# First mixer: q and k rotated through one gathered tile each, and scaled by 1/rms on eviction

## The chip, the cores and the metric

The kernel runs on one core of a Trainium2 chip. The metric is the time of one execution on the device in microseconds (us). Engines: TensorE (PE, matmuls; PEld its weight loads), VectorE (DVE), ScalarE (ACT), GpSimd (POOL), and SyncE (SP), which only issues transfers. ACTq is ScalarE's instruction queue. L1188 is line 1188 of the kernel before.

## What is computed

Two decoder layers over 512 tokens of width 1024, in float32. Each layer: token mixer, cross-attention into 256 memory tokens, SwiGLU feed-forward, each behind an RMS norm and with a residual. The first layer's mixer, cut to what matters:

```python
proj = h @ w_in                       # h: rms-normed input
x_br, y_br, q, k, v = jnp.split(proj, list(AB_SPLITS), axis=-1)
rec = rg_lru(causal_depthwise_conv(x_br, ...), ...) * jax.nn.gelu(y_br)
q = partial_rope(heads(q), cos, sin)  # 8 heads of 64; only the first 16 of a head's 64 rows turn
k = partial_rope(heads(k), cos, sin)
att = dilated_attention(q, k, heads(v))
return jnp.concatenate([rec, att], axis=-1) @ w_out

def partial_rope(x, cos, sin):        # ROT_DIM = 16, half = 8
    x1, x2 = x[..., :half], x[..., half:ROT_DIM]
    return concatenate([x1 * cos - x2 * sin, x2 * cos + x1 * sin, x[..., ROT_DIM:]])
```

## The kernel before

Activations lie transposed: 128 partitions of features, 512 columns of tokens. Every large product is done in three matmuls of 128x512 (`product`, L606, L609, L610): a float32 operand is split into a high and a low part, and high x high, high x low and low x high are summed. A weight unit (256 rows of 512 columns) is loaded by SyncE into one of four slots (L404), GpSimd writes its high part (L537), VectorE its low part (`low_part`, L1188). A unit's load waits until TensorE has begun the unit three before it. `low_to(u)` in VectorE's stream writes low parts up to unit u; where these calls stand is an order written out by hand. The engines run their streams in order and meet at semaphores only.

The norm's 1/rms is not applied to the input but behind the product, since it is one factor a token: `rstd` holds it for all 128 partitions.

Order of TensorE in the first mixer: in_x (two groups of four output tiles, 4 weight units each), in_q (one group: four tiles of q), four gate groups (one unit each; they need the convolved x in high and low parts, `conv` and `conv_low` on VectorE), the turning of the normed memory (L764), in_k, in_v (by token), then the mixer: 12 score steps, three for each of four pairs of heads, with halves of the y projection (`half_columns`) between them. PSUM has 8 banks: even-numbered groups use banks 0 to 3, odd ones 4 to 7, so a group waits until the one two before it has been read (`s_free`). in_q's banks are wanted by the second gate group, in_k's by the mixer.

q and k before: ScalarE copies each tile from PSUM unscaled (`raw_tiles`, L1892). VectorE turns each of the eight tiles by itself (`qk_tile`, `rotate`, L1255 to L1258: shuffle, times cosines, times sines, sum, each over 128 partitions, of which 32 change) with tables `cos_r` and `sin_r`, which are the cosines and sines times 1/rms (L1383, L1384) and hold 1 and 0 in the rows that don't turn, so that this also scales the tile. q's four tiles are turned between the gated products of the gates (`gated`, L1424); k's first two in the middle of the recurrence (`recur`, L1446 and L1447), the other two in mixer steps 1 and 4 (the score step of pair p waits only for tile p of k).

ScalarE's stream: the raw copies of q; per gate group two sigmoids for r (L1904) and two for i (L1907), the latter into two buffers that `gated` must have read; the memory's high parts; exponentials, tanh and roots of the decay; the raw copies of k; v's evictions (L1927); then the mixer's exponentials (L1946), copies and GeLUs.

The second layer rotates q and k in another way: ScalarE issues transfers that gather the 16 turning rows of each head into a packed tile, 32 rows a tile of q or k (L1995), VectorE turns the packed tile once (`rotate_pack`, L1560 to L1563) with tables in packed form that SyncE loads ahead of that layer, and ScalarE issues the transfers back (`spread`, L2006).

## Time and profile before

| | |
|---|---|
| time, median of 3 runs | 1348.42 us (1346.99 to 1348.92) |
| the profiled execution | 1347.47 us, span 1345.6 us |
| busy share of the span | PE 99%, PEld 81%, DVE 56%, ACT 26%, POOL 24% |
| granted TensorE clock | 1.0 over the run |
| moved by DMA | 129.85 MB, mean 96 GB/s |

The profile is of one execution. The page has the busy shares and the costliest groups of instructions; the trace behind it is asked for the timeline of one engine, its waits (who released it), the instructions of one line, and busy time by stretches. Spans are from the first instruction; about 1.9 us of the execution's time lie outside. A share of 99% on TensorE says that it is the engine to watch, and the few microseconds in which it waits say where.

### The profile page before, as it was taken

The page shows a single profiled execution, that of the slowest core. Times are in us where ns is not written, and L with a number is a line of the kernel's source. Part 1 is how long each engine was busy: PE and PEld are TensorE (multiplying, and loading weights), DVE is VectorE, ACT ScalarE, POOL GpSimd, SP SyncE. Part 2 cuts the span into 40 slices and gives each one's busy share as a digit, 9 for nine tenths or more (in the row PEclk, how much of TensorE's full clock was granted, in tenths as well). Part 3 has the DMA queues.
Part 4 walks back from the last instruction along what each step waited for, and adds up shares of the span by engine and source line. Part 5 has one row for each costly group of instructions (what it writes and reads, how often), then busy time and mean ns, then how long its engine had stood idle before and what let it go on. Part 6 is the DMA issues. An engine that isn't in the chain of part 4 may idle for free.

```text
span 1345.6 us, 17355 instructions
## 1 busy us (share of the span) xinstructions
PE 1329.2 (99%) x6432; PEld 1089.1 (81%) x6432; DVE 750.6 (56%) x1089; ACT 351.8 (26%) x733; POOL 321.8 (24%) x358
## 2 busy tenths in 40 slices
PE   8999999999999999999999999999999999999998
PEld 7877778888788888888888878888788888888886
DVE  6997975446685443234444668557674443334432
ACT  5338355312441110001111246523321110001112
POOL 2122125311421121111211126424222111122110
PEclk9999999999999999999999999999999999999999
DMA  6332222233333232233323341122323333333222
GB/s 208 102 95 79 94 70 76 78 104 93 108 95 101 94 94 94 98 104 95 94 94 112 99 128 57 64 95 82 106 94 94 94 96 104 99 94 94 94 94 94
DMA packets 95985, 129.85 MB, mean 96 GB/s; under 512 B 6416, under 2 KB 60944, under 8 KB 95920
## 3 DMA queue, kind: packets, MB, share of 16 engines
q1 hardware_dynamic: 94448, 127.31, 29.6%
q10 hardware_dynamic: 1472, 1.64, 0.5%
q8 instruction: 45, 0.74, 0.2%
q14 instruction: 20, 0.16, 0.0%
HBM read 125.19 MB, written 2.10 MB: 95 GB/s over the span
## 4 chain that ended last, share of the span: by engine, by line
PE 86%; DVE 8%; issue 2%; DMA 1%; POOL 1%; ACT 0%; SPq 0%; ACTq 0%; DVEq 0%; POOLq 0%
PE ps L606 24%; PE ps L609 24%; PE ps L610 24%; DVE xc L1389 1%; PE ps L1160 1%; PE ps L1156 1%; PE ps L1159 1%; DVE w_lo L1188 1%; DMA raw<-in_w_in 1%; PE ps L732 1%; PE ps L707 1%; PE ps L984 1%; PE ps L1002 1%; PE ps L1017 1%; DVE xc L1447 1%
## 5 line engine op out<-in xcount | busy, mean ns | idle before, releaser
L1188 DVE TENSOR_TENSOR w_lo<-raw,w_hi 128x1024 fp32r<-128x1024 f32 x226 | 281.6, 1246 | 425.5 <-POOL w_hi L537 423.9
L537 POOL TENSOR_SCALAR w_hi<-raw 128x1024 fp32r<-128x1024 f32 x226 | 249.9, 1106 | 922.5 <-DMA raw<-in_w_gate_up 403.3
L606 PE MATMUL ps<-z_hi,w_hi 128*128 128x512 f32 x1040 | 408.8, 393 | 3.3 <-ACTq L1910 1.8
L610 PE MATMUL ps<-z_hi,w_lo 128*128 128x512 f32 x1040 | 404.8, 389 | 0.0
L609 PE MATMUL ps<-z_lo,w_hi 128*128 128x512 f32 x1040 | 404.8, 389 | 0.0
L606 PEld LDWEIGHTS ps<-z_hi,w_hi 128*128 128x128 f32 x1040 | 195.2, 188 | 50.8 <-issue 8.3
L609 PEld LDWEIGHTS ps<-z_lo,w_hi 128*128 128x128 f32 x1040 | 195.3, 188 | 41.2 <-issue 1.4
L610 PEld LDWEIGHTS ps<-z_hi,w_lo 128*128 128x128 f32 x1040 | 195.2, 188 | 40.6
L606 PE MATMUL ps<-f_hi,w_hi 128*128 128x512 f32 x528 | 208.0, 394 | 1.8 <-issue 1.1
L610 PE MATMUL ps<-f_hi,w_lo 128*128 128x512 f32 x528 | 205.6, 389 | 0.0
L609 PE MATMUL ps<-f_lo,w_hi 128*128 128x512 f32 x528 | 205.5, 389 | 0.0
L2117 ACT ACTIVATE ff_g<-ff_g 128x512 f32<-128x512 f32 x44 | 27.7, 632 | 349.0 <-DVE ff_g L1710 349.0
L606 PEld LDWEIGHTS ps<-f_hi,w_hi 128*128 128x128 f32 x528 | 99.1, 188 | 24.0 <-issue 2.8
L609 PEld LDWEIGHTS ps<-f_lo,w_hi 128*128 128x128 f32 x528 | 99.2, 188 | 21.0 <-issue 1.0
L610 PEld LDWEIGHTS ps<-f_hi,w_lo 128*128 128x128 f32 x528 | 99.1, 188 | 20.9
L2120 ACT ACTIVATE f_hi<-ff_u 128x512 f32 (+1 forms) x44 | 27.2, 633 | 183.1 <-DVE ff_u L1721 183.1
L1768 ACT ACTIVATE z_hi<-h,vec 128x512 fp32r<-128x512 f32 x48 | 34.7, 722 | 128.2 <-DVEq L1228 127.1
L1202 DVE SCALAR_TENSOR_TENSOR z_lo<-h,vec,z_hi 128x512 fp32r<-128x512 f32 x48 | 38.9, 810 | 8.7 <-DVE h L1223 6.9
L1710 DVE TENSOR_TENSOR ff_g<-ps,rstd 128x512 f32<-128x512 f32 x44 | 30.2, 690 | 21.7 <-PE ps L610 21.4
L529 POOL TENSOR_SCALAR prob_window<-prob_window,stat 128x128 f32<-128x128 f32 (+1 forms) x64 | 32.9, 534 | 34.2 <-DVE stat L1584 34.2
L1223 DVE TENSOR_TENSOR h<-ps,h 128x512 f32<-128x512 f32 x48 | 33.0, 687 | 8.4 <-PE ps L610 7.2
L1208 DVE TENSOR_TENSOR acc<-acc,sq 128x512 f32<-128x512 f32 x42 | 33.0, 785 | 0.0
(211 smaller groups left out, 1295.1 us busy)
## 6 DMA issues: line engine op xcount, KB each, us to landing
raw<-in_w_gate_up SPq DMA_DIRECT2D x176, 256.0 KB
raw<-in_w_down SPq DMA_DIRECT2D x44, 512.0 KB
raw<-in_w_in SPq DMA_DIRECT2D x20, 512.0 KB
raw<-in_w_out SPq DMA_DIRECT2D x20, 512.0 KB
raw<-in_xa_wkv SPq DMA_DIRECT2D x16, 512.0 KB
raw<-in_w_in SPq DMA_DIRECT2D x16, 256.0 KB
raw<-in_xa_wq SPq DMA_DIRECT2D x8, 512.0 KB
raw<-in_xa_wo SPq DMA_DIRECT2D x8, 512.0 KB
```

The lines of the kernel that those rows point to most:

```text
L529: ins = pool.tensor_scalar(prob[:, c:c + w], prob[:, c:c + w], stat0[:, p % 3, 4, TB * e + i:TB * e + i + 1], 1.0, ALU.mult, ALU.mult)
L537: pool.tensor_scalar(w_hi[:, slot], raw[:, slot], 1.0, 1.0, ALU.mult, ALU.mult).then_inc(s_hi, 1)
L606: ins = pe.matmul(o, whi, rhi, start=start, stop=False)
L609: pe.matmul(o, whi, rlo, start=False, stop=False)
L610: return pe.matmul(o, wlo, rhi, start=False, stop=stop)
L1188: dve.tensor_tensor(w_lo[:, slot], raw[:, slot], w_hi[:, slot].bitcast(F32), ALU.subtract).then_inc(s_lo, 1)
L1202: dve.scalar_tensor_tensor(z_lo[:, m, :], h[:, m, :], v(f"g_{norm}", m), z_hi[:, m, :].bitcast(F32), ALU.mult, ALU.subtract).then_inc(s_zl, 1)
L1208: ins = dve.tensor_tensor(acc[:], acc[:], sq[:, m % 2, :], ALU.add)
L1223: ins = dve.tensor_tensor(h[:, m, :], ps[:, b, :], h[:, m, :], ALU.add)
L1710: dve.tensor_tensor(ff_g[:, p, :], ps[:, b0 + p, :], rstd[:], ALU.mult).then_inc(s_ff_gate, 1)
L1768: act.activation(dst[:, m, :], h[:, m, :], ACT.Identity, scale=v(f"g_{norm}", m)).then_inc(s_zh, 1)
L2117: act.activation(ff_g[:, p, :], ff_g[:, p, :], ACT.Silu).then_inc(s_ff_silu, 1)
```

## The change

q's and k's tiles are evicted from PSUM by VectorE times `rstd` (`scaled`, L1249; in place of ScalarE's raw copies and of the scaled tables, which go). ScalarE then issues eight transfers of 16 rows, two a tile, that gather the 128 turning rows of q (of k) into one tile `pack0`. VectorE turns that tile once with the packed tables, and ScalarE issues eight transfers that spread it back. The packed tables are loaded at the start, so the second loading before the second layer and its wait go, and the second layer's counters start from the first's. In VectorE's stream q's evictions stand ahead of the memory norm and its rotation behind it and one low part; k's evictions stand behind the decay and its rotation behind the first four recurrences. In ScalarE's stream q's gather stands where the raw copies stood and its spread behind the second gate group; k's gather and spread stand together ahead of v's evictions. The first score step waits for both spreads whole.

```diff
--- before.py
+++ after.py
@@ -79,6 +79,8 @@
 PACKS = ((0, 1, 2, 8), (3, 4, 5), (6, 7))
+PACK0 = 128
+SPREAD1 = (PACK0 + 224, PACK0 + 96, 64)
 
...
@@ -193,8 +195,7 @@
         rope0 = [at(f"rope0_{i}", [P, T], F32, z_fh + 2048 * (8 + i)) for i in range(2)]
-        cos_r = at("cos_r", [P, T], F32, z_fh + 2048 * 11)
-        sin_r = at("sin_r", [P, T], F32, z_fl + 2048 * 8)
+        pack0 = [at(f"pack0_{i}", [P, T], F32, o) for i, o in enumerate((z_fh + 2048 * 11, z_fl + 2048 * 8))]
         m0 = at("m0", [P, TB * P], F32, z_fl + 2048 * 11)
@@ -265,7 +266,7 @@
         s_tok_sum, s_tok_rms, s_tok = sem("s_token_sum"), sem("s_token_rms"), sem("s_token_rstd")
-        s_qk_raw = sem("s_qk_raw")
+        s_qk = sem("s_qk_scaled")
         s_rstd = sem("s_rstd")
@@ -276,7 +277,7 @@
         s_rec, s_rech, s_recl = sem("s_rec"), sem("s_rec_hi"), sem("s_rec_lo")
-        s_q0, s_v0 = sem("s_qk0"), sem("s_v0")
+        s_v0 = sem("s_v0")
         s_qkv1, s_qkv1b, s_q1_done = sem("s_qkv1"), sem("s_qkv1_biased"), sem("s_q1_done")
@@ -461,9 +462,6 @@
                 if l:
-                    sp.wait_ge(s_tok, 3)
-                    sp.dma_start(cos_t[:], rope_cos16).then_inc(s_rope, 16)
-                    sp.dma_start(sin_t[:], rope_sin16).then_inc(s_rope, 16)
                     stream("qkv_q0", w_qkv, 4)
@@ -862,8 +860,9 @@
                 p, c = divmod(s, 3)
-                if c == 0:
-                    pe.wait_ge(s_q0, 5 + p)
+                if s == 0:
+                    pe.wait_ge(s_spread[0], PACK0)
+                    pe.wait_ge(s_spread[1], PACK0)
                 if s:
@@ -973,7 +972,7 @@
                             pack_ = 0 if p < 3 else 1 if p < 6 else 2
-                            pe.wait_ge(s_spread[pack_], (224, 96, 64)[pack_])
+                            pe.wait_ge(s_spread[pack_], SPREAD1[pack_])
                         x_ = 2 * p + c
@@ -1249,13 +1248,14 @@
 
-            def rotate(dst, src, tmp, done_sem, cos=cos_t, sin=sin_t):
-
-                swap = list(range(8, 16)) + list(range(8)) + list(range(16, 32))
-                link(dve.stream_shuffle(tmp[0][:], src, swap))
-                dve.tensor_tensor(tmp[1][:], src, cos[:], ALU.mult)
-                link(dve.tensor_tensor(tmp[0][:], tmp[0][:], sin[:], ALU.mult))
-                dve.tensor_tensor(dst, tmp[1][:], tmp[0][:], ALU.add).then_inc(done_sem, 1)
+            def rotate(rows, tmp, tiles):
+
+                r = slice(0, 32 * tiles)
+                swap = list(range(8, 16)) + list(range(8)) + list(range(24, 32)) + list(range(16, 24))
+                link(dve.stream_shuffle(tmp[0][r, :], rows[r, :], swap))
+                dve.tensor_tensor(tmp[1][r, :], rows[r, :], cos_t[r, :], ALU.mult)
+                link(dve.tensor_tensor(tmp[0][r, :], tmp[0][r, :], sin_t[r, :], ALU.mult))
+                dve.tensor_tensor(rows[r, :], tmp[1][r, :], tmp[0][r, :], ALU.add).then_inc(s_rot, 1)
 
@@ -1379,9 +1379,6 @@
             dve.reciprocal(rms_tok[:, TB:], rms_tok[:, 0:TB]).then_inc(s_tok, 1)
-            dve.wait_ge(s_rope, 32)
-            dve.tensor_tensor(cos_r[:], cos_t[:], rstd[:], ALU.mult).then_inc(s_tok, 1)
-            dve.tensor_tensor(sin_r[:], sin_t[:], rstd[:], ALU.mult).then_inc(s_tok, 1)
 
@@ -1409,30 +1406,30 @@
                         conv_low(m - 2)
                     low_to(UNIT0["in_x"] + m0_ + {0: 7, 2: 8, 4: 9, 5: 10}.get(i, 0))
-            memory_norm(0)
-
-            def qk_tile(t):
-                n, x_ = t % 4, (q0, k0)[t // 4]
-                dve.wait_ge(s_qk_raw, t + 1)
-                dve.wait_ge(s_tok, 3)
-                if t:
-                    dve.wait_ge(s_q0, t)
-                rotate(x_[:, n, :], x_[:, n, :], rope0, s_q0, cos_r, sin_r)
+
+            def qk_scaled(x_, name):
+                for t in range(4):
+                    scaled(x_[:, t, :], GROUP0[name], t, s_done[name], t + 1)
+                    dve.nop().then_inc(s_qk, 1)
+
+            def qk_rotated(i):
+                dve.wait_ge(s_pack[i], PACK0)
+                rotate(pack0[i], rope0, 4)
 
             def gated(m):
 
             gates0 = UNIT0["gates"]
-            for t in range(4):
-                qk_tile(t)
-                if t:
-                    gated(2 * t - 2)
-                    gated(2 * t - 1)
-                low_to(gates0 + 3 + t)
-            gated(6)
-            gated(7)
-            low_to(gates0 + 7)
+            qk_scaled(q0, "in_q")
+            memory_norm(0)
+            low_to(gates0 + 3)
+            dve.wait_ge(s_rope, 32)
+            qk_rotated(0)
+            for hd in range(LRU_HEADS):
+                gated(2 * hd)
+                gated(2 * hd + 1)
+                low_to(gates0 + 4 + hd)
 
             def decay(m):
@@ -1465,11 +1462,12 @@
                 decay(m)
                 low_to(gates0 + {1: 9, 4: 10, 7: 11}.get(m, 0))
-            for m in range(4):
+            qk_scaled(k0, "in_k")
+            for m in range(3):
                 recur(m)
             low_to(gates0 + 12)
-            qk_tile(4)
-            qk_tile(5)
+            recur(3)
+            qk_rotated(1)
             low_to(gates0 + 13)
             for m in range(4, DB):
@@ -1529,8 +1527,6 @@
                 if s in (1, 3, 5, 7):
                     y_tile(s - 1)
-                if s in (1, 4):
-                    qk_tile(6 + s // 4)
                 if s < STEPS + 4:
                     low_to(mx_unit + s + 3)
@@ -1554,13 +1550,8 @@
 
-                        dve.wait_ge(s_pack[g], 32 * len(PACKS[g]))
-                        r = slice(0, 32 * len(PACKS[g]))
-                        swap = list(range(8, 16)) + list(range(8)) + list(range(24, 32)) + list(range(16, 24))
-                        link(dve.stream_shuffle(rope1[0][r, :], pack[g % 2][r, :], swap))
-                        dve.tensor_tensor(rope1[1][r, :], pack[g % 2][r, :], cos_t[r, :], ALU.mult)
-                        link(dve.tensor_tensor(rope1[0][r, :], rope1[0][r, :], sin_t[r, :], ALU.mult))
-                        dve.tensor_tensor(pack[g % 2][r, :], rope1[1][r, :], rope1[0][r, :], ALU.add).then_inc(s_rot, 1)
+                        dve.wait_ge(s_pack[g], (PACK0 if g < 2 else 0) + 32 * len(PACKS[g]))
+                        rotate(pack[g % 2], rope1, len(PACKS[g]))
 
@@ -1600,7 +1591,6 @@
                     qkv1(v1_t[:], s_done["qkv_kv"], "qkv_kv", 1, 2)
-                    dve.wait_ge(s_rope, 64)
                     rotate_pack(0)
@@ -1885,15 +1875,21 @@
                         act.activation(f_hi[:, m - 1, :], xc[:, m - 1, :], ACT.Copy).then_inc(s_xch, 1)
 
-            def raw_tiles(dst, name, told):
-                g = GROUP0[name]
+            def qk_gathered(i, x_):
                 for t in range(4):
-                    act.wait_ge(s_done[name], t + 1)
-                    act.activation(dst[:, t, :], ps[:, bank(g, t), :], ACT.Copy).then_inc(s_qk_raw, 1)
-                act.wait_ge(s_qk_raw, told)
-                act.nop().then_inc(s_free[g % 2], 4)
-
-            raw_tiles(q0, "in_q", 4)
+                    act.wait_ge(s_qk, 4 * i + t + 1)
+                    for e in range(2):
+                        act.dma_start(pack0[i][32 * t + 16 * e:32 * t + 16 * e + 16, :],
+                                      x_[HD * e:HD * e + 16, t, :]).then_inc(s_pack[i], 16)
+
+            def qk_spread(i, x_):
+                act.wait_ge(s_rot, i + 1)
+                for t in range(4):
+                    for e in range(2):
+                        act.dma_start(x_[HD * e:HD * e + 16, t, :],
+                                      pack0[i][32 * t + 16 * e:32 * t + 16 * e + 16, :]).then_inc(s_spread[i], 16)
+
+            qk_gathered(0, q0)
             act.wait_ge(s_sp, 1)
 
@@ -1908,6 +1904,8 @@
                 act.wait_ge(s_act, 2 * hd + 2)
                 act.nop().then_inc(s_free[g % 2], 4)
+                if hd == 1:
+                    qk_spread(0, q0)
             memory_high(0)
             act.wait_ge(s_gx, DB)
@@ -1919,7 +1917,8 @@
                 act.wait_ge(s_lq, m + 1)
                 act.activation(lru_r[:, m, :], lru_r[:, m, :], ACT.Sqrt).then_inc(s_ls, 1)
-            raw_tiles(k0, "in_k", 8)
+            qk_gathered(1, k0)
+            qk_spread(1, k0)
             act.wait_ge(s_tok, 1)
             g_v = GROUP0["in_v"]
...
...
@@ -2177,16 +2176,10 @@
     cos, sin = np.cos(ang).T, np.sin(ang).T
-    cos_t, sin_t = np.ones((P, T), np.float32), np.zeros((P, T), np.float32)
-    for head in (0, HD):
-        for half in range(2):
-            r = head + half * rot // 2
-            cos_t[r:r + rot // 2] = cos
-            sin_t[r:r + rot // 2] = sin if half else -sin
     cos16, sin16 = np.tile(cos, (P // (rot // 2), 1)), np.tile(np.concatenate([-sin, sin]), (P // rot, 1))
     root_hd = np.float32(HD ** 0.5)
-    return dict(mask0=mask0 * root_hd, mask1=mask1 * root_hd, rope_cos=cos_t, rope_sin=sin_t,
-                rope_cos16=cos16.astype(np.float32), rope_sin16=sin16.astype(np.float32), identity=np.eye(P, dtype=np.float32))
+    return dict(mask0=mask0 * root_hd, mask1=mask1 * root_hd, rope_cos=cos16.astype(np.float32),
+                rope_sin=sin16.astype(np.float32), identity=np.eye(P, dtype=np.float32))
 
```

## Rows read from the trace of the kernel before

**Rows 1.** The page, part 1: busy us (share of the span) xinstructions
```profile
PE 1329.2 (99%) x6432; PEld 1089.1 (81%) x6432; DVE 750.6 (56%) x1089; ACT 351.8 (26%) x733; POOL 321.8 (24%) x358
```

**Rows 2.** TensorE's waits, whole run: waited for: us in total, times, longest
```profile
PE ps L606 <- ACTq L1910: 1.8, 1, 1.8
...
PE ps L873 <- DVE stat L1488: 1.5, 1, 1.5
...
PE ps L606 <- issue: 1.1, 1, 1.1
...
PE ps L606 <- DVEq L1521: 0.7, 1, 0.7
```

**Rows 3.** Timeline, TensorE: start us, us, line op xcount [idle before, releaser]
```profile
85.57 0.47 PE L606 MATMUL ps<-f_hi,w_hi 128*128 128x512 f32 x1 [1.11 <-issue]
...
111.12 0.50 PE L606 MATMUL ps<-z_hi,w_hi 128*128 128x512 f32 x1 [1.76 <-ACTq L1910]
...
154.87 0.93 PE L873 MATMUL ps<-k,q 64*128 64x128 f32 x8
...
162.99 0.92 PE L873 MATMUL ps<-k,q 64*128 64x384 f32 x4 [1.52 <-DVE stat L1488]
```

**Rows 4.** Timeline, VectorE, 40 to 162 us
```profile
40.88 0.66 DVE L1383 TENSOR_TENSOR cos_r<-cos_t,rstd 128x512 f32<-128x512 f32 x1
...
83.40 2.07 DVE L1188 TENSOR_TENSOR w_lo<-raw,w_hi 128x1024 fp32r<-128x1024 f32 x1
...
87.31 1.42 DVE L1265 TENSOR_SCALAR mem_nat<-mem_nat,small 128x1024 f32<-128x1024 f32 x2
...
88.65 0.73 DVE L1255 STREAM_SHUFFLE rope<-q 128x512 f32<-128x512 f32 x1
...
132.90 1.23 DVE L1188 TENSOR_TENSOR w_lo<-raw,w_hi 128x1024 fp32r<-128x1024 f32 x1 [1.85 <-POOL w_hi L537]
...
144.68 0.73 DVE L1255 STREAM_SHUFFLE rope<-k 128x512 f32<-128x512 f32 x1
...
150.26 0.69 DVE L1258 TENSOR_TENSOR k<-rope,rope 128x512 f32<-128x512 f32 x1
...
160.60 1.22 DVE L1188 TENSOR_TENSOR w_lo<-raw,w_hi 128x1024 fp32r<-128x1024 f32 x1
```

**Rows 5.** Timeline, ScalarE, 91 to 111 us
```profile
91.38 1.28 ACT L1904 ACT_TABLE_LOAD   x1 [5.88 <-PE ps L610]
...
109.16 0.69 ACT L1907 ACTIVATE gate_i<-ps,vec 128x512 f32<-128x512 f32 x1 [0.82 <-DVE xc L1424]
...
110.32 0.69 ACT L1907 ACTIVATE gate_i<-ps,vec 128x512 f32<-128x512 f32 x1
```

**Rows 6.** VectorE: one eviction (timeline), then three lines: ns min/median/max, first and last
```profile
767.97 0.69 DVE L1249 TENSOR_TENSOR q<-ps,rstd 128x512 f32<-128x512 f32 x1 [0.24 <-DVE q L1249]
...
L1249 DVE TENSOR_TENSOR xpad<-ps,rstd x8: 678/684/692, 42.1 to 76.1; 128x512 f32<-128x512 f32 x8
L1446 DVE TENSOR_TENSOR lru_r<-lru_r,xc x8: 684/692/1353, 134.0 to 158.6; 128x512 f32<-128x512 f32 x8
L1447 DVE TENSOR_TENSOR_SCAN xc<-lru_a,lru_r x8: 1224/1225/1225, 134.8 to 159.3; 128x512 f32<-128x512 f32 x8
```

**Rows 7.** Second layer: the packed rotation (timeline), then the spread's DMA issues by line
```profile
779.26 0.73 DVE L1560 STREAM_SHUFFLE rope<-pack 128x512 f32<-128x512 f32 x1
...
781.36 0.69 DVE L1563 TENSOR_TENSOR pack<-rope,rope 128x512 f32<-128x512 f32 x1
...
L2006 ACTq DMA_DIRECT2D q<-pack x16: 514/611/618, 782.1 to 837.2; - x16
...
DMA to landing us min/median/max: 1.9/2.1/4.0
```

**Rows 8.** End by windows: stretch, busy PE, PEld, DVE, ACT, POOL, PEclk, DMA, GB/s
```profile
1342.00:1344.00 2.00, 0.00 (x0) 0.00 (x0) 0.49 (x1) 0.53 (x1) 0.00 (x0) 1.00 0.31 118
1344.00:1345.60 1.60, 0.00 (x0) 0.00 (x0) 0.00 (x0) 0.00 (x0) 0.00 (x0) 0.61 0.49 181
```

More of the change, by code:

```diff
@@ L135, in trunk @@
 def trunk(nc, x, mem, w_in, w_gates, w_out0, w_qkv, w_out1, xa_wq, xa_wkv, xa_wo, w_gate_up, w_down,
-          vectors, gains, mask0, mask1, rope_cos, rope_sin, rope_cos16, rope_sin16, identity, out):
+          vectors, gains, mask0, mask1, rope_cos, rope_sin, identity, out):
     ctx = ExitStack()
@@ L1998, in spread @@
                     def spread(g):
-                        act.wait_ge(s_rot, g + 1)
+                        act.wait_ge(s_rot, 2 + g + 1)
                         for t in PACKS[g]:
@@ L2038, in q_biased @@
                         if t == 6:
-                            act.wait_ge(s_spread[0], 224)
+                            act.wait_ge(s_spread[0], SPREAD1[0])
                         gather(t, n)
```

## The prediction, made before the changed kernel was run

> **What bounds the kernel now.** The page's first part shows TensorE at work for 99% of the span [rows 1]. Its matmuls are pipelined, so this alone proves little, but their spacing agrees: from 111.12 to 154.87 us it runs the 192 matmuls of in_k and in_v, 0.228 us each, without a break [rows 3]. Time can be won only where TensorE stands still, or lost by making it stand still. The second view is therefore the list of TensorE's own waits over the run. Three of its entries, 4.4 us together, lie between 84 and 163 us, the stretch that the change touches; behind them in the mixer stands one more, of 0.7 us [rows 2]. The timeline puts the three in place [rows 3]:
> - gap A, 1.11 us before 85.57: the first gate group needs the low half of its weights, a subtraction on VectorE that runs from 83.40 to 85.47 [rows 4].
> - gap B, 1.76 us before 111.12: in_k needs the banks of the last gate group. ScalarE reads them with four activations, the second of which had waited 0.82 us for a gated product of VectorE; the last ends at 111.01 [rows 5].
> - gap C, 1.52 us before 162.99: the second score step needs the maxima of the first on VectorE, which starts them after a weight subtraction at 160.60 to 161.8 [rows 4].
>
> So behind all three stands VectorE, which is about full here. The third view is its timeline. After 163 us TensorE has no gap in the mixer but the one of 0.7 us at its end [rows 2], so what VectorE does there (the rotations of k tiles 2 and 3 at mixer steps 1 and 4) costs nothing, and taking it away gains nothing.
>
> **The change part by part.** My clock is the start of the second score step, 162.99 us; whatever moves it moves the end, since TensorE is unbroken behind it.
>
> *Scaled tables go.* Two multiplications at 40.9 to 42.1 us, 1.2 us with the step between them [rows 4]. VectorE is in a closed chain (convolution, evictions, weight subtractions) up to 87 us, so all of that comes 1.2 us earlier: the subtraction of gap A ends near 84.2, TensorE is free at 84.3. Gap A goes: -1.1 us, and gate group 0 runs 84.4 to 89.9 (24 matmuls x 0.228).
>
> *q's eviction moves from ScalarE to VectorE.* Four scaled evictions, each 0.69 us plus 0.24 us for the wait on itself, 0.93 us [rows 6], so 3.7 us from 85.9 to 89.65. Gate group 1 needs these banks at 89.9. It just fits; every delay of VectorE by more than 0.2 us is a wait of TensorE. GpSimd's weight pass falls here too. A two-input operation in SBUF is held up by it (one multiplication of the recurrence took 1353 ns against a median of 692), while the evictions from PSUM never were (678 to 692 ns in eight) [rows 6], so I charge nothing. The Trainium skill (SBUF — State Buffer, Who interferes with whom) says the same of a VectorE instruction with at most one SBUF input; had it been otherwise this stage would lose some 0.6 us.
>
> *q's gather, rotation and spread.* ScalarE issues eight small transfers, each 0.61 us of its queue [rows 7]: 4.9 us, from 86.7 to 91.6, behind which its gate activations wait. TensorE's gate group 0 ends at 89.9, so ScalarE is 1.7 us late for it: table load (1.28 us [rows 5]) and four activations end at 95.3, and gate group 2 wants those banks at 95.4. No wait, no slack. The last gather lands 2.1 us after its issue, near 93; VectorE has the memory norm (1.4 us [rows 4] and a short reciprocal) and one weight subtraction (1.2 us) until 92.4, then waits 0.6 us, rotates in 2.8 us (779.26 to 782.05 in the second layer, the same four instructions on a full tile [rows 7]) and does the gated products from 95.8. Four tile rotations, of which the first begins at 88.65 [rows 4], become one. The eight issues of the spread stand on ScalarE from 98.3 to 103.3; gate group 2 ends at 100.9, so its activations end at 105.8, and TensorE needs those banks at 106.4. Only the activations of the last gate group remain in front of in_k: TensorE ends it at 106.4, four activations of 0.6 us follow without the former 0.82 us wait, and in_k starts at 109.2 instead of 111.12. Gap B shrinks to about 1 us. Sum so far: -1.9 us. Bounds: if the gathers land after 4.0 us, the longest of the nearest rows [rows 7], in place of 2.1, everything behind slips, and in_k starts at 110.3 (-0.8); if the evictions are late by the whole 1.2 us as well, -0.3.
>
> *k's path.* VectorE's weight subtraction at 132.90 is tied to TensorE (its weights are loaded when an earlier unit begins), so it comes 1.9 us earlier and ends near 132.2. Before, from 134.04 to the end of the subtraction at 161.8 VectorE had 27.7 us of work, of which 6.3 us were two k rotations (144.68 to 150.95 [rows 4]). Now it has four evictions (3.7) and one rotation (2.8) in their place: 0.2 us more. The eviction was ScalarE's before; the path got longer. The packed k rotation ends behind four evictions, four recurrences (0.69 and 1.23 us [rows 6] and a step between, 1.98), one subtraction of 1.2 us and two hold-ups by GpSimd's weight passes, 0.66 us each (1353 less 692 ns): 132.2 + 3.7 + 7.9 + 1.2 + 1.3 + 2.8 = 149.1. The gathers (ScalarE free near 133.9, the last landing at 140.5) are hidden under the recurrences.
>
> *The new wait.* Scores need the whole spread. ScalarE issues it behind the rotation: first issue at 149.1, the eighth seven steps of 0.63 us later (0.61 [rows 7] and a little between), landing 2.1 us after that: 155.6, scores 0.1 us behind. TensorE is ready at 154.87 - 1.9 = 153.0. It stands still for 2.7 us. This is where most of the gain goes. Then the first score step and its half of the y projection follow, which took 6.44 us (154.87 to 161.31, the end before gap C [rows 2, 3]): 162.15. The maxima are ready by then: after 149.1 come a subtraction (1.2), four recurrences (7.9), a hold-up (0.7), a subtraction (1.2) and the 1.2 us that lay between its end and 162.99 before, so 161.3. Gap C is gone, swallowed by the new one. Also behind the spread on ScalarE's queue: v's evictions, from 154.1 to 156.7, needed only by the turns of step 4.
>
> *Without effect.* ScalarE's eight raw copies; the tables' second loading in front of the second layer, with its wait on SyncE and its place in the weight queue (TensorE never waits there for weights); raised thresholds of the shared semaphores, long reached.
>
> **Sum.** -1.1 (A), -0.8 (B), -1.5 (C), +2.7 (new wait before the scores): -0.7; by the clock 162.99 to 162.15, -0.8. The profiled execution took 1347.47 us, 1.87 more than its span of 1345.6; it would take 1346.7. It lies 0.95 below the median of the runs shown, so the forecast for the median is 1347.6 us. A difference of 0.2% (2.7 us) is about the least that a measurement of this kernel can tell from no change.
>
> **Rivals.**
> 1. *Issues are cheap or overlap.* The Trainium skill (DMA: Bandwidth & Descriptors, Issuing engines are not separate DMA queues) calls the sequencer's time for a transfer usually small beside the transfer itself. Rows speak against it: 0.61 us each, one after the other, against 2.1 us to land [rows 7]. If the eight spreads left at once, k would be there near 151.3, before TensorE; then VectorE's maxima at 161.3 bound the second step: -1.7, 1346.7 us.
> 2. *The k spread comes late (slower).* The one place is the chain rotation, eight issues, landing, scores. It has no cover: 1 us later is 1 us of time. It turns the sign from a slip of 0.8 us. If q's gathers take their 4.0 us (+1.1) and the last spread as well (+1.9), the second step starts at 165.15: +2.2, 1350.6 us. For it: a landing of 4.0 us exists [rows 7]. Against: the last spreads fall into a stretch without weight loads, since TensorE stands and asks for none.
> 3. *q's eviction holds gate group 1.* If the 1.2 us of the scaled tables don't come through to 87 us, its banks are free only at 91: gap A returns one group later, +1.1, so 1348.7 us.
> 4. *The clock falls.* A stand of 2.7 us is longer than any in this stretch before. At the end of the run the granted clock was still 1.00 from 1342 to 1344, 2 us without a single matmul, and fell only in the last slice [rows 8]; so it should hold. If it fell to the half (1.2 of 2.4 GHz) for 5 us (no row here says how long; I take about twice the stand), half of them are lost: +2.5, so 1350.1 us. The Trainium skill (TensorE: Matmul & The Clock Gate, Part 1) also has the clock halved after idling and given back after sustained work.
> 5. *The wait isn't there and neither is gap B*: VectorE gains more from the fewer rotations than I see, all three gaps close: -3.5, 1344.9 us.
>
> **How the numbers follow.** Forecast 0.60; rival 1 0.10; rival 2 0.12; rival 3 0.10; rival 4 0.03; rival 5 0.05. All but rival 5, and parts of rivals 2 and 4, lie within 0.2% of 1348.42: faster 0.06, same 0.86, slower 0.08. The range leaves out rival 5 at the lower end; above it reaches to the middle of rival 2 and most of rival 4: 1345.8 to 1350.2.
>
> **What would show it.** Right: in the profile after, no wait before the first gate matmul; in_k starts 1.5 to 2 us earlier; VectorE waits up to 1 us for the q gather; TensorE has one wait of 2 to 3.5 us before the first scores, released by a transfer from the packed tile to k; none at the second score step. Wrong: a wait before gate groups 1 or 2, issues much shorter than 0.6 us, a new TensorE wait later in the mixer because v's evictions or exponentials stand behind the issues, or a granted clock under 1.00 near 156 us.

## The result, and the profile after

The changed kernel takes 1349.72 us (median of 20 runs, 1347.51 to 1352.71), the kernel before 1347.62 us on the same chip (median of 20). The ratio is 1.0013, 95% interval 1.0008 to 1.0019. On a second chip it was 1.0020 (1.0012 to 1.0029). By these ratios the change costs 1.8 to 2.7 us. Forecast was a gain of 0.8. Either is about 0.2% or less, but the sign was wrong, and both intervals leave out 1.

The profiled execution took 1349.26 us with a span of 1347.5. First the page's first part and, below it, TensorE's own waits (waited for: us in total, times, longest), which answer [rows 1, 2]. Line numbers are from here on those of each run's own kernel: L604 here is L606 of the kernel before, L872 its L873.

```profile
PE 1331.5 (99%) x6432; PEld 1090.2 (81%) x6432; DVE 734.0 (54%) x1065; ACT 347.3 (26%) x725; POOL 320.4 (24%) x358
...
PE ps L872 <- DMA k<-pack: 2.6, 1, 2.6
...
PE ps L983 <- DMA k<-pack: 0.6, 1, 0.6
PE ps L604 <- ACTq L1906: 0.5, 1, 0.5
...
PE ps L762 <- ACTq L1906: 0.3, 1, 0.3
```

VectorE has lost 16.6 us of work, and TensorE's matmuls are the same in number, yet take 2.3 us more. The three gaps of [rows 3] are gone or small, 0.8 us in place of 4.4. In their place stands one wait of 2.6 us. By this list alone the kernel would be faster. TensorE's timeline (start, duration, line, tiles, count, idle before) puts them in place, against [rows 3]:

```profile
106.25 1.94 PE L762 MATMUL ps<-ident,mem_nat 128*128 128x128 f32 x16 [0.26 <-ACTq L1906]
...
108.72 0.50 PE L604 MATMUL ps<-z_hi,w_hi 128*128 128x512 f32 x1 [0.53 <-ACTq L1906]
...
155.13 1.65 PE L872 MATMUL ps<-k,q 64*128 64x128 f32 x8 [2.58 <-DMA k<-pack]
...
163.20 0.92 PE L872 MATMUL ps<-k,q 64*128 64x384 f32 x4
```

in_k starts at 108.72 instead of 111.12, and the second score step has no wait before it. Still it starts at 163.20, not at 162.99 or earlier. The first score step, 0.93 us before, took 1.65 us. The reason is in the view by windows (stretch; its length, busy PE, PEld, DVE, ACT, POOL; the granted clock; DMA share, GB/s):

```profile
152.00:155.00 3.00, 0.55 (x3) 0.13 (x1) 2.90 (x4) 1.28 (x3) 0.43 (x1) 1.00 0.20 45
155.00:158.00 3.00, 2.87 (x11) 2.05 (x12) 2.93 (x3) 2.43 (x3) 0.00 (x0) 0.51 0.00 0
158.00:159.00 1.00, 1.00 (x4) 0.77 (x4) 0.96 (x2) 0.00 (x0) 0.00 (x0) 0.77 0.24 52
```

After the stand (so I call a time in which TensorE waits) TensorE runs at its lower level of 1.2 GHz for about 3.4 us. This stretch and a second one in the second layer, which is taken up below, are where the same matmuls took longer. The first of them eats what the vanished gap C gave.

**A ruler for all runs.** Profiles start at slightly different places, so I measure from the start of the first matmul of the norm's sum (30.75 us before, 30.52 after; in_k after: 108.72 - 30.52 = 78.20). "Mixer's end" is the start of the first matmul behind the short wait there, 237.77 in the first profile of either kernel. All are worked out from the timeline of TensorE; "stand" is its idle time ahead of the first scores, "half clock" the stretch up to the mixer's end in which the granted clock was half. A row that begins with "and" adds its edit to the row above; the edits are shown below.

| kernel, profile | in_k | stand | first scores | second step | mixer's end | half clock |
|---|---|---|---|---|---|---|
| before | 80.37 | 0 | 124.12 | 132.24 | 207.02 | none |
| before, second | 80.61 | 0 | 124.36 | 132.35 | 207.10 | none |
| changed | 78.20 | 2.58 | 124.61 | 132.68 | 207.25 | after the stand |
| changed, second | 80.56 | 2.62 | 126.99 | 135.10 | 209.65 | after the stand |
| 22 fillers | 78.27 | filled | 126.93 | 133.49 | 208.08 | none |
| tile 0 alone | 81.16 | 0 | 124.90 | 133.00 | 207.57 | none |
| 12 fillers | 80.54 | filled | 126.99 | 133.55 | 208.13 | none |
| q's spread late | 79.45 | 2.92 | 126.18 | 134.33 | 208.90 | after the stand |
| tile 0 and q late | 79.56 | 0 | 123.34 | 131.73 | 207.87 | after second step |
| tables loaded again | 78.05 | 2.38 | 124.28 | 132.43 | 207.00 | after the stand |
| k rotated early | 80.63 | 0 | 124.40 | 132.68 | 207.24 | none |
| and last scan behind | 80.97 | 0 | 124.73 | 131.26 | 205.84 | none |
| and q's spread late | 79.63 | 0 | 123.37 | 129.90 | 204.48 | 32 to 35.4 us, before in_k |
| before, last scan behind | 80.23 | 0 | 125.59 | 132.12 | 206.88 | after in_k's wait |

What lies behind the mixer's end, up to the end of the span, took 1107.7 to 1111.3 us in these fourteen profiles: 1107.8 and 1110.1 in the two of the kernel before, 1109.7 and 1108.3 in the two of the changed one. So a single profile's time says less than the ruler, and no loss behind the mixer shows that would belong to the change.

### The profile page after: what moved, and what is told of

The parts are those of the page before. It is cut to its first block, busy times and chain, and to the rows that moved or that the text cites. A ratio compares the mean times of both kernels' runs of the same rounds, so it can differ in the third digit from the quotient of the medians.

```text
span 1347.5 us, 17356 instructions
## 1 busy us (share of the span) xinstructions
PE 1331.5 (99%) x6432; PEld 1090.2 (81%) x6432; DVE 734.0 (54%) x1065; ACT 347.3 (26%) x725; POOL 320.4 (24%) x358
## 4 chain that ended last, share of the span: by engine, by line
PE 88%; DVE 4%; ACTq 2%; ACT 2%; issue 2%; DMA 1%; POOL 1%; SPq 0%; DVEq 0%; POOLq 0%
PE ps L604 25%; PE ps L608 25%; PE ps L607 25%; PE ps L1159 1%; PE ps L1158 1%; PE ps L1155 1%; PE ps L730 1%; PE ps L705 1%; PE ps L983 1%; DVE w_lo L1187 1%; PE ps L1001 1%; PE ps L1016 1%; ACTq L1889 1%; PE ps L872 1%; PE ps L803 1%
## 5 line engine op out<-in xcount | busy, mean ns | idle before, releaser
L604 PE MATMUL ps<-z_hi,w_hi 128*128 128x512 f32 x1040 | 409.8, 394 | 1.7 <-DVE z_lo L1201 1.1
L604 PEld LDWEIGHTS ps<-z_hi,w_hi 128*128 128x128 f32 x1040 | 195.7, 188 | 49.5 <-issue 8.1
L604 PE MATMUL ps<-f_hi,w_hi 128*128 128x512 f32 x528 | 207.9, 394 | 0.7 <-DVEq L1519 0.7
L604 PEld LDWEIGHTS ps<-f_hi,w_hi 128*128 128x128 f32 x528 | 99.1, 188 | 22.3 <-issue 1.3
```

Source lines behind the costliest of these rows:

```text
L604: ins = pe.matmul(o, whi, rhi, start=start, stop=False)
```

## The experiments

Runs sent together share a chip and the runs of the kernel before: the first four 1347.29 us (28 runs), the next four 1346.73 (27), the last four 1347.91 (35).

### Both kernels again

> The kernel before once more, for a second profile. Theory B as a rule of the change: no stretch of lowered clock before the tail. Rival (the clock falls in the second layer of either kernel, by the phase of the chip's counting): a stretch at half clock near 793 us can show here too, and the time is then 1.3 us longer than in the first profile, 1348.8.

> The changed kernel once more, on the chip of the next three, as their measure and for a second look at its profile. Theory A (clock): the stand of 2.6 us before the first scores halves the granted clock for one stretch of 3.4 us in the first mixer in most executions, costing 1.6 us, and the first mixer then ends where it ended before. Theory B (second layer): the 1.9 us of the profile come from the second layer, where an issue of ScalarE that met an instruction fetch slipped the spread by 0.6 us and a second stretch at half clock cost 1.3. If both are rules and no accident: 1.001 to 1.002 of the time before, and both low stretches are in this profile again. If the second is an accident of one execution, it is missing here.

The kernel before, profiled again (1348.85 us), shows the three gaps at 1.2, 1.9 and 1.4 us: its pattern repeats. The half clock near 793 us, which its first profile hadn't, shows here too, as the rival said. The changed kernel, 1350.02 us (11 runs), repeats the stand (2.62 us) and the half clock behind it, but neither the low stretch of the second layer (theory B falls: it is no rule of the change) nor the early in_k. The two profiles of the changed kernel differ by 2.36 us at in_k and by 2.40 at the mixer's end. VectorE's timeline of the second:

```profile
86.12 0.68 DVE L1248 TENSOR_TENSOR q<-ps,rstd 128x512 f32<-128x512 f32 x1
...
94.77 0.01 DVE L1255 LOAD_MASK_SELECT rope<-pack  x1 [2.18 <-DMA pack<-q]
94.80 0.75 DVE L1255 STREAM_SHUFFLE rope<-pack 128x512 f32<-128x512 f32 x1
```

and that of the first:

```profile
82.14 0.68 DVE L1248 TENSOR_TENSOR q<-ps,rstd 128x512 f32<-128x512 f32 x1
...
89.55 0.01 DVE L1255 LOAD_MASK_SELECT rope<-pack  x1 [0.95 <-DMA pack<-q]
```

So there are an early form and a late form of the gate stage. Between 31 and 86 us VectorE's 24 convolution steps took 19.8 us in the first profile and 20.7 in the second, the eight low parts of f 5.5 and 7.2, the ten weight subtractions 12.2 and 13.9: GpSimd's weight passes meet other instructions. (In the second profile, for instance, a low part of f at 83.52 takes 1.54 us instead of 0.68 while a pass of GpSimd runs from 82.47 to 84.53.) Behind it, in the late form, stands this on ScalarE:

```profile
98.25 0.69 ACT L1903 ACTIVATE gate_i<-ps,vec 128x512 f32<-128x512 f32 x1 [1.54 <-DVE xc L1421]
...
100.24 5.50 ACTq L1889 DMA_DIRECT2D q<-pack  x8
105.80 0.69 ACT L1900 ACTIVATE lru_r<-ps,vec 128x512 f32<-128x512 f32 x1 [5.69 <-PE ps L608]
```

The rotation of q is late, so a gated product is late, so a sigmoid waits 1.54 us, so the eight issues of q's spread start at 100.24 and hold the third gate group's sigmoids to 105.80. TensorE pays with 1.26 us before the memory turning and 0.54 before in_k; with 0.22 and 0.51 before the second and third gate groups that is 2.5 us, against the 2.9 us of gaps A and B in the kernel before. Of the kernels here whose q part is as in the changed one, the late form is in five profiles (in_k at 80.5 to 81.2), the early one in three (78.05 to 78.3).

### Filling the stand: 22 fillers

```diff
@@ mixer_scores, s == 0 @@
+                    for _ in range(22):
+                        pe.matmul(ps[:, mx["k_banks"][1], 0:P], ones[:], ones[:], start=True, stop=True)
                     pe.wait_ge(s_spread[0], PACK0)
                     pe.wait_ge(s_spread[1], PACK0)
```

> The changed kernel with 22 matmuls of ones (128x128, about 0.11 us each, 2.4 us) into an unused bank while TensorE waits for k's spread. Theory A: no lowered clock near 156 us, the second score step starts at 161.6 instead of 163.2, 1.6 us less than the changed kernel. Rival (the stand itself costs all and the clock nothing): same time as the changed kernel.

Measured: 1350.78 us, ratio 1.0023 (1.0014 to 1.0032); not faster. The clock stayed at 1.00 from 150 to 163 us, and from the first scores to the second step passed 6.56 us instead of 8.07. But the fillers ran for 5.07 us, until 156.51, while the last issue of the spread had ended at 152.71. So they held the scores up themselves: from the start of the stage's last matmul to the first scores passed 5.23 us, against 2.96 in the changed kernel. The balance by the ruler is +2.3 - 1.5 = +0.8 us, and the mixer ends 0.83 later than in the changed kernel's early form. The experiment was mis-sized; it shows the half clock's cause, the stand, but not its price in time. This profile also has waits of its own in the second layer, 1.9 us for q's last spread and a half clock from 842 us, which I can't put down to the fillers.

### The right number: 12 fillers

```diff
-                    for _ in range(22):
+                    for _ in range(12):
```

> The changed kernel with 12 small fp32 matmuls of ones by ones (written to a bank that is cleared anyway, results unused) in TensorE's queue ahead of the wait for k's spread. In the run with 22 of them the fillers took 5.07 us (0.23 each), from 151.51 to 156.51, while the last issue of the spread ended at 152.71, so they held the first scores up by about 2 us themselves. Twelve take 2.8 us, about the length of the stand (2.58 and 2.62 us). Theory A, the stand costs twice, by its length and by the half clock that follows it (3.4 us at 0.50, about 1.6 us lost): the clock stays at 1.00 from 150 to 165, the first scores start within 0.5 us of where they start without fillers, measured from the end of the stage before them, the second score step comes 1.6 us earlier than in the changed kernel, and the time is 1.0 to 2.0 us less than the changed kernel's. Theory B, the half clock is given back before the mixer ends, since the end of the mixer stood at the same place with and without it: second step earlier, time within 0.5 us of the changed kernel's.

TensorE and the clock by windows, 155 to 158 us, then TensorE's timeline:

```profile
155.00:158.00 3.00, 3.00 (x30) 2.88 (x31) 2.90 (x4) 2.10 (x4) 0.00 (x0) 1.00 0.15 33
```

```profile
154.83 2.84 PE L865 MATMUL ps<-ones 128*128 128x128 f32 x24
157.60 0.93 PE L874 MATMUL ps<-k,q 64*128 64x128 f32 x8
...
164.16 0.92 PE L874 MATMUL ps<-k,q 64*128 64x384 f32 x4
```

It is of the late form, and to be held against the changed kernel's second profile: first scores at the same 126.99, second step 1.55 us earlier, mixer's end 1.52 earlier. The half clock costs 1.5 us, and theory B (given back before the end) falls. The time was 1348.91 us, ratio 1.0011 (1.0002 to 1.0020), against 1.0020 and 1.0013 of the changed kernel: the direction fits, the size isn't separable in the times.

### Waiting for k's tile 0 alone

```diff
-SPREAD1 = (PACK0 + 224, PACK0 + 96, 64)
+SPREAD1 = (PACK0 + 224, PACK0 - 32 + 96, 64)
...
-                    pe.wait_ge(s_spread[1], PACK0)
+                    pe.wait_ge(s_first, 32)
+                if s == 3:
+                    pe.wait_ge(s_spread[1], PACK0 - 32)
@@ qk_spread @@
-                                      ...).then_inc(s_spread[i], 16)
+                                      ...).then_inc(s_spread[i] if i == 0 or t else s_first, 16)
```

> The changed kernel, but the first scores wait only for the two transfers that spread k's tile 0, on a semaphore of their own; the other six are waited for at the second pair of heads. Tile 0 lands near 151.3, before TensorE is ready at 152.4, so the wait of 2.6 us and the lowered clock behind it go. The maxima of the first step end at 160.6, so the second step starts at 160.7 instead of 163.2: 2.5 us less than the changed kernel, 1.5 to 2.3 less than before if the second layer is as before. Rival (the spread is not what holds the mixer, VectorE is): the second step no earlier than 162.

1347.52 us, ratio 0.9994 (0.9985 to 1.0003), 2.5 us less than the changed kernel on the same chip. The profile shows no stand before the first scores, and gap C is back:

```profile
155.32 0.93 PE L875 MATMUL ps<-k,q 64*128 64x128 f32 x8
...
163.42 0.92 PE L875 MATMUL ps<-k,q 64*128 64x384 f32 x4 [1.50 <-DVE stat L1489]
```

So, as far as the times can tell, the loss of the changed kernel is the stand before the first scores with what follows it. Everything else in the change comes to nothing measurable in this (late) form: the mixer ends at 207.57, against 207.02 and 207.10 before.

### q's spread behind k's gathers, alone and with tile 0

```diff
                 if hd == 1:
-                    qk_spread(0, q0)
...
             qk_gathered(1, k0)
+            qk_spread(0, q0)
             qk_spread(1, k0)
```

> The changed kernel with the eight issues of q's spread moved on ScalarE's queue from between gate groups 1 and 2 to behind k's eight gathers, where the engine is idle for some 9 us (139.7 to 148.6) and from where q still lands before the first scores. Theory A, the issues of q's spread (5.5 to 5.9 us on the queue, one of them stretched to 1.2 to 1.5 us beside an instruction fetch) hold up gate group 2's sigmoids and through them the banks of the memory turning: its start moves from 1.3 to 2.0 us late to 0.3 or less late, in_k's start to 108.2 to 109.5 even where q's gather lands late, and the time falls by 0 to 1.5 us against the changed kernel; the stand before the first scores keeps 2.6 us. Theory B, the gates wait for the multiplications on VectorE (xc) and not for the issues: the waits ahead of the memory turning and of in_k keep their 0.5 to 2 us and the time doesn't move.

> The changed kernel with k's tile 0 on a semaphore of its own, as before (first scores wait for two of k's eight transfers only), and with q's spread behind k's gathers. If the two losses are separate, this takes both away: no low clock in 150 to 165, at most 1.5 us idle before the second score step, in_k 1 to 2.4 us earlier than in the kernel before, and a time of 0 to 1.5 us below the run with tile 0 alone, so 0.5 to 2 us below the kernel before (ratio 0.9985 to 0.9996). If what is won ahead of in_k is spent again in the k chain, the time stays within 0.5 us of the run with tile 0 alone (ratio 0.9994).

Alone: 1349.22 us, ratio 1.0012 (1.0003 to 1.0021). With tile 0 as well: 1346.78 us, ratio 0.9996 (0.9987 to 1.0005). In both the memory turning has no wait any more, and TensorE waits 0.83 us before in_k:

```profile
107.19 1.91 PE L762 MATMUL ps<-ident,mem_nat 128*128 128x128 f32 x16
...
109.94 0.50 PE L604 MATMUL ps<-z_hi,w_hi 128*128 128x512 f32 x1 [0.83 <-ACTq L1906]
...
156.67 0.93 PE L872 MATMUL ps<-k,q 64*128 64x128 f32 x8 [2.92 <-DMA k<-pack]
```

The issues of q's spread cost 1.1 us of in_k in the late form (79.45 against 80.56 by the ruler), though the gathers still land late and VectorE waits 2.3 us for them. Of this 0.3 us went into a longer stand, 2.92 us: k's chain doesn't move with TensorE by the full amount. In the run with both, gap C is 1.79 us and the clock falls behind it (0.51 from 163 to 166), which costs some 1.6 us (76.1 us from the second step to the mixer's end, 74.6 with tile 0 alone); the first scores were 1.5 us earlier than with tile 0 alone, the mixer's end 0.3 later. So whether the two gains add up could not be seen there.

### The tables loaded again

```diff
                 if l:
+                    sp.wait_ge(s_rot, 2)
+                    sp.dma_start(cos_t[:], rope_cos).then_inc(s_rope, 16)
+                    sp.dma_start(sin_t[:], rope_sin).then_inc(s_rope, 16)
...
+                    dve.wait_ge(s_rope, 64)
                     rotate_pack(0)
```

> The changed kernel with the two table loads restored to the SP queue at the head of the second layer, as the kernel before has them (here they load the same tables again). Theory A, without those loads the instruction fetch near 775 meets an issue of ScalarE's spread instead of an issue of SP: with them the wait of the window's first scores for the spread is 0.1 us or less and the stretched issue (1.19 us at 775.4) is back to 0.6. Theory B, the fetch follows ScalarE's own instruction stream, which is changed by the 32 issues of the first mixer: the wait stays 0.3 to 0.6 us with the loads restored.

A single run, 1347.07 us, of the early form. The wait of the second layer is as long as without the loads:

```profile
PE ps L986 <- DMA k<-pack: 0.6, 1, 0.6
```

Theory A falls. And the second profile of the kernel before has this wait too (0.5 us), where the first had none. It isn't the change's. The same holds for the half clock near 793 us in the changed kernel's first profile, since the kernel before has it in its second one (and the last version below in its profile, 0.50 from 790 to 792 us):

```profile
792.00:796.00 4.00, 3.88 (x13) 2.73 (x14) 3.40 (x14) 1.55 (x3) 0.00 (x0) 0.57 0.17 29
```

### Rotating k earlier

```diff
-            for m in range(3):
+            for m in range(2):
                 recur(m)
             low_to(gates0 + 12)
-            recur(3)
             qk_rotated(1)
+            recur(2)
+            recur(3)
```

> The changed kernel with k's packed rotation two scans (one product and one scan each, about 2.0 us) earlier in VectorE's order: it stands behind recurrences 0 and 1 and the weights' low part, with recurrences 2 and 3 behind it. In the changed kernel the rotation of k ended at 148.6 (150.1 in the run with q's spread late), though k's gather had landed some 5 us before it began. Theory A, the stand before the first scores is VectorE's order and not the transfers themselves: the rotation ends some 4 us earlier, the eight issues (5.0 us) follow at once, the spread lands before the v stage ends, the wait of 2.6 us is gone, the clock stays at 1.00 there, and in place of it the second score step waits 1.2 to 1.8 us for the maxima on VectorE, as in the kernel before, since VectorE has the same work ahead of them. Time 2 to 3 us less than the changed kernel, so about that of the kernel before (ratio 0.9985 to 1.0000). Theory B, the transfers or ScalarE's queue set it: the wait keeps 1.5 us or more.

1347.08 us, ratio 0.9989 (0.9981 to 0.9998). Theory A holds in each part. VectorE and ScalarE, then TensorE:

```profile
142.73 0.74 DVE L1255 STREAM_SHUFFLE rope<-pack 128x512 f32<-128x512 f32 x1
...
144.89 0.69 DVE L1258 TENSOR_TENSOR pack<-rope,rope 128x512 f32<-128x512 f32 x1
...
145.62 5.00 ACTq L1890 DMA_DIRECT2D k<-pack  x8
```

```profile
154.06 0.93 PE L872 MATMUL ps<-k,q 64*128 64x128 f32 x8
...
162.34 0.92 PE L872 MATMUL ps<-k,q 64*128 64x384 f32 x4 [1.68 <-DVE stat L1487]
```

The spread is issued by 150.6 and has landed when TensorE arrives. The transfers themselves are as before; what made the stand was two recurrences, 4 us, in front of the rotation on VectorE. Gap C is back with 1.68 us.

### The last recurrence behind the maxima, in the changed kernel and in the one before

```diff
-            for m in range(4, DB):
+            for m in range(4, DB - 1):
                 recur(m)
...
                     mixer_maxima(s)
+                if s == 0:
+                    recur(DB - 1)
```

> As e7_rotate_early, and VectorE's last recurrence (a product and a scan, 2.0 us) is moved behind the maxima of the first score step. Theory A, the wait of the second score step is VectorE's queue ahead of the maxima: with neither stand left, the second score step starts 6.6 to 6.8 us after the first (8.1 in the kernel before), and the time falls by another 1.0 to 1.5 us: ratio 0.9975 to 0.9990. Theory B, something else is late next there (the weights' high or low part, ScalarE's exponentials): less than 0.5 us is won.

> The kernel before with one thing of e8: VectorE's last recurrence behind the maxima of the first score step. If the 1.5 us stand before the second score step (1.52 and 1.40 us in its two profiles) is VectorE's queue and nothing else, it is gone here without packing anything: 1.2 to 1.5 us less than the kernel before, ratio 0.9989 to 0.9991. If it is bound to how k is rotated, it stays.

On top of the early rotation: 1346.33 us, 0.9988 (0.9980 to 0.9997). In the kernel before: 1346.46 us, 0.9988 (0.9980 to 0.9997). In both the wait before the second step is gone:

```profile
155.15 0.93 PE L872 MATMUL ps<-k,q 64*128 64x128 f32 x8
...
161.68 0.92 PE L872 MATMUL ps<-k,q 64*128 64x384 f32 x4
```

```profile
156.35 0.93 PE L873 MATMUL ps<-k,q 64*128 64x128 f32 x8
...
162.88 0.92 PE L873 MATMUL ps<-k,q 64*128 64x384 f32 x4
```

6.53 us from one step to the next in either, as where the clock was held up by fillers (6.56). Gap C was VectorE's queue and had nothing to do with how k is rotated. On the changed side the gain of 1.4 us shows in the ruler (205.84 against 207.24), while the times moved by 0.75 us, which they can't resolve. In the kernel before the profile fell on a half clock of 3.4 us behind in_k's wait of 1.92 us:

```profile
112.00:115.00 3.00, 3.00 (x9) 2.28 (x8) 2.73 (x5) 2.98 (x7) 0.00 (x0) 0.52 0.63 175
```

### All three together

This version has the early rotation, the last recurrence behind the maxima, and q's spread behind k's gathers; that is, the two edits above and

```diff
-                if hd == 1:
-                    qk_spread(0, q0)
...
             qk_gathered(1, k0)
+            qk_spread(0, q0)
```

> As e8_and_recur7, and q's spread stands behind k's gathers on ScalarE's queue, as in e4. k's spread then follows q's: in e4 q's eight issues ended at 143.6, with the rotation at 145.6 or later, so k's are not held. It brought in_k 1.1 us earlier in e4 than the late form of the changed kernel. Theory A: that 1.1 us is kept, now that the chain of k has slack: ratio to before 0.9965 to 0.9985. Theory B: k's chain is late again by some of it, a wait of 0.5 us or more stands before the first scores, and the time is that of e8.

1345.11 us, ratio 0.9979 (0.9970 to 0.9988), 2.8 us below the kernel before: this version beats both. What is left of the waits in the first mixer up to its last step:

```profile
109.67 0.50 PE L604 MATMUL ps<-z_hi,w_hi 128*128 128x512 f32 x1 [0.83 <-ACTq L1909]
...
153.41 0.93 PE L872 MATMUL ps<-k,q 64*128 64x128 f32 x8
...
159.94 0.92 PE L872 MATMUL ps<-k,q 64*128 64x384 f32 x4
```

Theory A holds in this: the 1.3 us at in_k against the version without the late spread (79.63, 80.97) are still there at the mixer's end (204.48, 205.84), and the times differ by 1.2 us. That the late spread alone gave these 1.3 us can't be read from this pair of profiles. The one with it is of the early form (VectorE waits 0.94 us for q's gather, against 2.34), which works for it, and had a half clock before in_k, which works against it:

```profile
32.00:35.00 3.00, 3.00 (x9) 2.32 (x8) 2.68 (x10) 0.84 (x2) 0.00 (x0) 0.50 0.00 0
```

Against the kernel before with its last recurrence moved (0.9988) packing is ahead by 0.9 thousandths, about 1.2 us; their intervals (0.9970 to 0.9988, 0.9980 to 0.9997) overlap. The two versions also differ in where q's spread stands, which only the packed one has. So that the packing itself pays is likely and not shown by the times.

## Why the prediction was wrong, point by point

In short: the new wait came as forecast. What failed is the gain before in_k (-1.9 us, A and B together), which the late form doesn't have, and the clock behind the new wait, which stood in the sum at nothing and cost 1.5 us.

*Gap A, -1.1: right.* No wait stands before the first gate matmul in either profile of the changed kernel. VectorE was even 4 us earlier in the early form. It is not sure in every execution: both profiles with q's spread late, which differ from the changed kernel only behind this point, have 0.57 and 0.66 us there.

*q's evictions from 85.9, no charge for GpSimd: right* in the late form (86.12 to 89.6), 0.2 us of wait before gate group 1.

*Gap B shrinks, in_k 1.9 us earlier: the first step that failed.* Against the kernel before, in_k came 2.2 us earlier in the early form and not at all in the late one, which is the more frequent here (five of eight). So in the late form gap A's 1.1 us was lost again on the way to in_k, and B's 0.8 never came. Two terms were too small. The rotation of q waited 2.18 us for its gather, not 0.6: it began at 94.8 where I had 93, because the last gather landed some 3.3 us after its issue began (94.77 less 91.5) and not the median of 2.1, which it did take in the early form (89.55 less 87.5). And the eight issues of q's spread took 5.5 and 5.9 us, with one stretched to 1.1 and 1.5 us, not 4.9 to 5.0, with no slack behind them, as the text itself said ("No wait, no slack"). The bound of 4.0 us for a landing was in the text, but only with a small weight and an in_k at 110.3; 110.9 came (111.3 if it is laid on the scale of the profile before by the ruler). A chain with no slack anywhere should have been forecast at its late bound. Moving q's spread behind k's gathers brought in_k back by 1.1 us of these, which shows that about half of it was the issues' place on ScalarE.

*The wait before the first scores, +2.7: right* in place, releaser and size: 2.58 and 2.62 us. But the text took the recurrences ahead of the rotation as given. Moving two of them took the wait away.

*Gap C, -1.5: right that the wait goes, wrong that the time comes back: the second step that failed.* From the first scores to the second step I had 6.5 us; it was 8.07 and 8.11, since the clock fell to half behind the stand. This is rival 4, which had 0.03 and a price of 2.5 us. It happened in all four profiles with a stand over 2.3 us, at 1.5 us. The reading that spoke against it, [rows 8], was of the end of the run, two us without a matmul at full clock. It was no witness. The same trace has its last matmul at 1340.07 and the clock at 1.00 up to 1344, but then at half:

```profile
1340.07 0.39 PE L1160 MATMUL ps<-w_hi,f_lo 128*128 128x512 f32 x1
...
1344.50:1345.50 1.00, 0.00 (x0) 0.00 (x0) 0.00 (x0) 0.00 (x0) 0.00 (x0) 0.50 0.26 96
```

So the clock did fall behind a stand, only some time after it had begun. In the mixer too it fell only when the stand was over or nearly so: about when the scores started in the changed kernel's first profile (155.13), and with q's spread late not before 158 us, though the scores started at 156.67. Full clock during a stand therefore says nothing of the clock behind it. The Trainium skill (TensorE: Matmul & The Clock Gate, Part 1) names the mechanism, a clock halved after idling, and the trace agrees: 0.51 from 155 to 158 us, behind the 2.58 us without a matmul.

*Without effect: right, as far as it was looked at.* The second layer's wait and its half clock occur in the kernel before too, and restored loads change nothing.

*The sum* by forms, from the terms measured: late 0 (A and B) + 2.6 (stand) - 1.5 (C) + 1.5 (clock) = +2.6, and the ruler has 209.65 against 207.06, +2.6; early -2.3 + 2.6 - 1.5 + 1.5 = +0.3, and the ruler has 207.25 and 207.00 against 207.06. The times, +1.8 and +2.7 us, fit a mixture of the two. That they are one is not shown, since only profiles tell the forms apart. Rivals 1, 3 and 5 did not occur: issues took 0.61 us one after the other, gate group 1 waited 0.2 us at most, and the gaps did not close. Rival 2 neither, for k; its mechanism, a late landing, struck at q. (Rival 5's -3.5 doesn't match its own text: the three gaps add up to 4.4.)

What stays open: what decides whether VectorE meets GpSimd's weight passes in the early or the late form, and what makes the clock fall behind some stands near 1.8 to 2.0 us and not behind others (below).

## What to carry to other kernels

Where a change gathers the work of several pieces into one, ask what the first consumer now waits for, and what stands in the producer's queue ahead of that one piece: here three small edits of the order (two recurrences behind the rotation, one behind the maxima, a spread where its engine is idle) were worth more than the packing, and turned a loss of 1.8 to 2.7 us into a gain of 2.8. A stand of TensorE is priced at its length plus the matmuls at half clock behind it, and a chain forecast as "just in time" at two places in a row is to be priced late.

## What the runs showed of the hardware

- Behind every stand of 2.38 to 2.92 us before the first scores (four profiles) TensorE's granted clock was half for 3.4 us, which cost 1.5 us. Filled with small matmuls of no use, the same stretch stayed at 1.00. Of shorter stands of TensorE in the first mixer, the clock fell behind one of 1.79 and one of 1.92 us, and not behind such of 1.40, 1.50, 1.52, 1.68, 1.69, 1.76, another of 1.92 and one of 1.96 us. So length alone doesn't decide. In single profiles it fell behind less: behind stands of 0.5 and 1.05 us with 1.5 us of matmuls between them near 790 us (in three profiles of the fourteen: the second of the kernel before, the first of the changed one, the one of all three edits together), and behind 1.04 us before the norm's sum in the last of these, where the others had 0.85 to 1.15 us without a fall.
- One DMA issue on ScalarE's queue took 514 to 618 ns, but single ones of q's spread 1119 and 1467 ns. At the longest, in the changed kernel's first profile at 99.5 us, the DMA queues of 98 to 101 us (packets, MB, share) show an instruction fetch:

```profile
q8 instruction: 1, 0.02, 2.7%
```

  Whether the one stretches the other was not tried.
- The same chain of VectorE instructions came out 4 us apart at q's first eviction (82.14 and 86.12 us) in two profiles of the same kernel. Single instructions that overlapped a pass of GpSimd took 0.65 to 0.86 us longer (a low part of f 1.54 us instead of 0.68, a weight subtraction 2.07 instead of 1.21).
